# Neighbourhood attention over 16x8 column blocks with a bias laid out by the host

## The reference

```python
GRID_W, WIN_COLS, rows = 64, 16, 8        # 512 tokens are a grid of 8 rows x 64 columns; 16 heads of 64
q, k, v, g = split(h @ w_in)              # latent tokens; kc, vc from the context tokens
row_idx = clip(r - 4, 0, rows - 8)[:, None] + arange(8)      # with 8 rows: always all 8
col_idx = clip(col - 8, 0, 64 - 16)[:, None] + arange(16)    # 16 neighbouring columns
s_loc = q . k[row_idx, col_idx] + rpb[head, row_idx - r + 7, col_idx - col + 15]
s_ctx = q . kc
p = softmax(concat(s_loc, s_ctx))         # over 128 neighbours and 256 context tokens
o = p_loc . v[row_idx, col_idx] + p_ctx . vc
y = (o * silu(g)) @ w_out
```

## Time and profile before

| | us |
|---|---|
| median of 3 runs | 3138.78 (3133.11 to 3140.57) |
| the profiled execution: its time | 3141.7 |
| the profiled execution: its span | 3139.9 |
| PE busy | 2919.9 (93%) |
| DVE busy | 1757.9 (56%) |
| ACT busy | 970.3 (31%) |
| POOL busy | 803.6 (26%) |

### The profile page before, as it was taken

How to read it: one execution, slowest core, us unless ns; L and a number is a source line. 1 busy time by engine, 2 the same in 40 slices (tenths; PEclk the granted TensorE clock), 3 DMA queues, 4 the chain that set the end, 5 groups by cost and what they waited for, 6 DMA issues and landing times. The chain is left out here.

```text
span 3139.9 us, 37990 instructions
## 1 busy us (share of the span) xinstructions
PE 2919.9 (93%) x14938; PEld 2410.3 (77%) x14938; DVE 1757.9 (56%) x2601; ACT 970.3 (31%) x1552; POOL 803.6 (26%) x304
## 2 busy tenths in 40 slices
PE   7999999999998898888989999999999889999999
PEld 6776777777777776667868888888888668878887
DVE  4984766666645998976556566552233536431111
ACT  2223344444332222223234423122222334332222
POOL 0221212111134443431200022232222120134444
PEclk8998999999999999899989999999999899999999
DMA  5244332232124553432310033331111120022223
GB/s 209 84 148 122 99 93 92 73 99 73 65 101 168 167 168 113 142 114 73 104 58 1 1 101 108 119 104 64 63 61 61 46 81 1 21 74 94 96 98 101
DMA packets 110896, 287.38 MB, mean 92 GB/s; under 512 B 38720, under 2 KB 41888, under 8 KB 110208
## 3 DMA queue, kind: packets, MB, share of 16 engines
q1 hardware_dynamic: 108560, 281.03, 27.0%
q10 hardware_dynamic: 2160, 3.93, 0.4%
HBM read 278.90 MB, written 6.03 MB: 91 GB/s over the span
## 5 line engine op out<-in xcount | busy, mean ns | idle before, releaser
L705 POOL TENSOR_TENSOR w_lo<-w_raw,w_hi 128x1024 fp32r<-128x1024 f32 x300 | 803.4, 2679 | 2325.2 <-ACT w_hi L987 2325.1
L753 PE MATMUL turns<-h_hi,w_hi 128*128 128x512 f32 (+1 forms) x2480 | 811.0, 376 | 86.5 <-POOL w_lo L705 67.9
L753 PE MATMUL turns<-h_hi,w_lo 128*128 128x512 f32 (+1 forms) x2480 | 786.4, 366 | 0.0
L753 PE MATMUL turns<-h_lo,w_hi 128*128 128x512 f32 (+1 forms) x2480 | 784.0, 366 | 0.0
L753 PEld LDWEIGHTS turns<-h_hi,w_hi 128*128 128x128 f32 x2480 | 428.3, 194 | 202.7 <-POOL w_lo L705 89.4
L1204 DVE CUSTOM_DVE_ANT_0 ada_acc<-ada_raw,cond_rows,ada_bias 128x1024 f32<-128x1024 f32 x264 | 501.2, 1923 | 19.3 <-DMA ada_raw<-in_adapack 11.6
L753 PEld LDWEIGHTS turns<-h_hi,w_lo 128*128 128x128 f32 x2480 | 424.0, 193 | 76.3
L753 PEld LDWEIGHTS turns<-h_lo,w_hi 128*128 128x128 f32 x2480 | 425.4, 193 | 73.2 <-issue 1.4
L987 ACT ACTIVATE w_hi<-w_raw 128x1024 fp32r<-128x1024 f32 x300 | 315.4, 1051 | 407.0 <-PE turns L753 389.0
L1195 DVE SCALAR_TENSOR_TENSOR x_lat<-turns,modulation,x_lat 128x512 f32<-128x512 f32 x112 | 83.9, 749 | 413.7 <-PE turns L753 413.7
L753 PE MATMUL turns<-m_hi,w_lo 128*128 128x512 f32 (+1 forms) x768 | 233.4, 358 | 0.0
(11 more groups left out here) (199 smaller groups left out, 3585.1 us busy)
## 6 DMA issues: line engine op xcount, KB each, us to landing
w_raw<-in_wpack SPq DMA_DIRECT2D x300, 512.0 KB, 3.5
ada_raw<-in_adapack SPq DMA_DIRECT2D x176, 512.0 KB, 4.4
bias<-bias_table SPq DMA_DIRECT2D x32, 224.0 KB, 3.8
ada_first_a<-in_adapack SPq DMA_DIRECT2D x12, 512.0 KB, 8.7
bias_table<-bias_out ACTq DMA_DIRECT2D x16, 240.0 KB, 2.4
x_lat<-in_xT SPq DMA_DIRECT2D x1, 2048.0 KB, 8.6
x_ctx<-in_ctxT SPq DMA_DIRECT2D x2, 1024.0 KB, 8.8
ada_first_b<-in_adapack SPq DMA_DIRECT2D x4, 512.0 KB, 14.7
```

What stands on the lines that cost most here:

```text
L705: pool.tensor_tensor(Wl[:, b, :], RAW[:, b, :], Wh[:, b, :].bitcast(F32), ALU.subtract).then_inc(w_split, 1)
L753: ins = pe.matmul(dst[:, lo:lo + sz], w, x[:, lo:lo + sz], start=first and n == 0, stop=last and n == 2)
```

## The change

1. The q, k, v and g tiles of the NA layer are evicted in another token order: four column blocks, each 8 rows x 16 columns = 128 tokens (`by_rows` is the old order read, `by_cols` the new order written, runs of 16 elements). q and g take a copy more on ACT, through `tmp1`; k and v are evicted in two instructions for latent and context. The output goes back to row order when it is written to `o_hi`, `o_lo`.
2. A query tile is now a column block, and meets only the blocks that its windows reach: `NA_CHUNKS` gives 2 local blocks + 2 context chunks for tiles 0 and 3, 3 + 2 for tiles 1 and 2. Scores, softmax, transposes and P*V go over 512 or 640 keys and not over 768; in P*V a block that only one of the two query tiles meets is multiplied over 128 queries.
3. Context and local scores lie side by side, and the bias holds zeros for the context, so that one DVE instruction adds, negates and takes the minimum (that is, minus the maximum), and one ACT instruction takes the exponential and its sum.
4. The bias comes from the host in its final layout, 128 x 1792 floats per head. The 16 `bias_row` steps, the HBM table, the loads of `onehot` and `rpb` and all waits on them are gone. The load of a head is one transfer of 896 KB; before it was two of 224 KB. No other work takes the place of the `bias_row` steps between the `poolmix` steps.
5. `ada_acc` loses its second half: `bias1` gets a home of its own. In `cond_rows` the two condition rows pass one after the other through the one buffer; the thrown-away product of `ada_chunk` goes on top of `ada_raw`; for the first sections the context accumulator lies in the arena.

```diff
+NA_CHUNKS = ((4, 5, 0, 1), (4, 5, 0, 1, 2), (4, 5, 2, 3, 1), (4, 5, 2, 3))
+NA_PLACE = ((0, 1, 4, 5), (0, 1, 2, 4, 5), (4, 5, 1, 2, 3), (4, 5, 2, 3))
+NA_BIAS_AT, NA_BIAS_W = (0, 896, 256, 1280), 1792
...
-                if L == 0:
-
-                    for _ in range((0, 2, 2, 2, 2, 2, 3, 3)[m]):
-                        add("bias_row", g=len(rows) // 8, c=len(rows) % 8, st=len(rows) % 2, k=len(rows) + 1)
-                        rows.append(1)
...
+        def by_cols(ap):
+            return ap.rearrange("p (b r c) -> p r b c", b=4, r=ROWS, c=WIN)
+        def by_rows(ap):
+            return ap.rearrange("p (r b c) -> p r b c", b=4, r=ROWS, c=WIN)
+        def score_at(qt):
+            local = (len(NA_CHUNKS[qt]) - 2) * P
+            return (TX - local, TX - local, TX) if qt < 2 else (TX - TC, TX, TX - TC)
...
-                if s is last_gate0:
-                    sp.wait_ge(dve_done, s.d1)
-                    sp.dma_start(HOT[:], A["onehot"]).then_inc(hot_in, 16)
-                    sp.dma_start(RPB[:], A["rpb"]).then_inc(hot_in, 16)
...
-                        for r in range(2):
-                            sp.dma_start(BIAS[n % 2][r * 64:r * 64 + 64, :].rearrange("c (s j) -> c s j", j=GRID_W),
+                        sp.dma_start(BIAS[n % 2][:], A["bias"][n]).then_inc(bias_in[n % 2], 16)
...
+                        if s.na:
+                            _, at_l, at_c = score_at(s.qt)
+                            k0, nl = min(c for c in NA_CHUNKS[s.qt]) * P, (s.nk - 2) * P
+                            pe.matmul(SP_[:, 0, at_l:at_l + nl], x[:, q], y[:, k0:k0 + nl], start=n == 0, stop=n == 2)
+                            ins = pe.matmul(SP_[:, 0, at_c:at_c + TC], x[:, q], y[:, TX:TT], start=n == 0, stop=n == 2)
...
+                        wide = NA_CHUNKS[s.qt + 1 if s.qt == 0 else s.qt]
+                        for n, k in enumerate(wide):
+                            q = slice(0, 256) if n < 4 else slice(P, 256) if s.qt == 0 else slice(0, P)
+                            for j, (v, p) in enumerate(((Vh, PTh[0]), (Vh, PTl[0]), (Vl, PTh[0]))):
+                                ins = pe.matmul(PS[:, b, TT + q.start:TT + q.stop], v[:, k, :], p[:, n, q], start=n + j == 0,
...
                     for c in range(2):
-                        ins = act.activation(ACC[:, c, :], CROW[:, c, :], ACT.Tanh, scale=0.5)
-                    ins.then_inc(crow_tanh, 1)
+                        if c:
+                            act.wait_ge(crow_made, 2 * n - 1)
+                        act.activation(ACC[:], CROW[:, c, :], ACT.Tanh, scale=0.5).then_inc(crow_tanh, 1)
...
-                            act.activation(ex[:, 0:TX], ex[:, 0:TX], ACT.Exp, bias=st[:, 2:3], scale=1.0, accum_out=st[:, 3:4])
-                            give(act.activation(ex[:, TX:TT], SP_[:, 0, TX:TT], ACT.Exp, bias=st[:, 2:3], scale=1.0,
-                                                accum_out=st[:, 4:5]))
+                            give(act.activation(ex[:, 0:nk], ex[:, 0:nk], ACT.Exp, bias=st[:, 2:3], scale=-1.0,
+                                                accum_out=st[:, 3:4]))
...
-                        give(act.activation(Oh[r, s.tile, s.q0:s.q0 + 256], PVT[r, :], ACT.Copy))
+                        give(act.activation(blocks(Oh[r, s.tile, :], s.q0), paired(PVT[r, :]), ACT.Copy))
...
-                        give(act.activation(G2[:, s.pair % 2, :], ps[:, 0:t], ACT.Tanh, scale=0.5))
+                        act.activation(by_cols(T1[:, 0:TX]), by_rows(ps[:, 0:TX]), ACT.Copy)
+                        give(act.activation(by_cols(G2[:, s.pair % 2, :]), by_rows(ps[:, 0:t]), ACT.Tanh, scale=0.5))
...
+                        if s.ev == "k":
+                            act.activation(dst[:, TX:TT], ps[:, TX:TT], ACT.Copy)
+                            give(act.activation(by_cols(dst[:, 0:TX]), by_rows(ps[:, 0:TX]), ACT.Copy))
+                        else:
+                            chain(act.activation(by_cols(T1[:, 0:TX]), by_rows(ps[:, 0:TX]), ACT.Copy, scale=0.125))
+                            give(act.activation(dst[:, 0:TX], T1[:, 0:TX], ACT.Copy))
...
-                            dve.tensor_tensor_reduce(ex[:, 0:TX], SP_[:, 0, 0:TX], bias, 1.0, -3.0e38, ALU.add, ALU.max,
-                                                     st[:, 0:1])
-                            chain(dve.tensor_reduce(st[:, 1:2], SP_[:, 0, TX:TT], AX.X, ALU.max))
-                            give(dve.tensor_scalar(st[:, 2:3], st[:, 0:1], st[:, 1:2], -1.0, ALU.max, ALU.mult))
+                            give(dve.tensor_tensor_reduce(ex[:, 0:nk], SP_[:, 0, s0:s0 + nk], bias, -1.0, 3.0e38, ALU.add, ALU.min,
+                                                          st[:, 2:3]))
...
-                        if s.na:
-                            chain(tt(st[:, 5:6], st[:, 3:4], st[:, 4:5], ALU.add))
-                            chain(dve.reciprocal(st[:, 6:7], st[:, 5:6]))
+                        chain(dve.reciprocal(st[:, 6:7], st[:, 3:4]))
```

More of the change, by code:

```diff
@@ L205, in na_scores @@
     def na_scores(n, q, k):
-        sc[n] = add("scores", na=True, pair=n // 8, half=n % 8 // 4, qt=n % 4, st=0, eb=n % 2, first=n % 4 == 0, nk=NT)
+        sc[n] = add("scores", na=True, pair=n // 8, half=n % 8 // 4, qt=n % 4, st=0, eb=n % 2, first=n % 4 == 0, nk=len(NA_CHUNKS[n % 4]))
         sc[n].after = [q, k]
     def na_trans(n):
-        tr[n] = add("trans", na=True, eb=n % 2, col=n % 2 * P, nk=NT, qt=n % 4)
+        tr[n] = add("trans", na=True, eb=n % 2, col=n % 2 * P, nk=len(NA_CHUNKS[n % 4]), qt=n % 4)
         tr[n].after = [soft[n - 1]]
@@ L468, in plan @@
     for s in steps:
-        n = {"hnorm": 0, "back": 0, "rope": 1, "vtrans": 1, "scores": s.st, "bias_row": s.st, "trans": 1 if s.na else None}.get(s.kind)
+        n = {"hnorm": 0, "back": 0, "rope": 1, "vtrans": 1, "scores": s.st, "trans": 1 if s.na else None}.get(s.kind)
         if n is not None:
@@ L590, in build_blocks @@
         act_own, dve_own = sem("act_own"), sem("dve_own")
-        consts_in, x_in, hot_in = sem("consts_in"), sem("x_in"), sem("hot_in")
-        bias_out = [sem(f"bias_out{n}") for n in range(2)]
+        consts_in, x_in = sem("consts_in"), sem("x_in")
         bias_in = [sem(f"bias_in{n}") for n in range(2)]
@@ L801, in _ @@
                     unit(s)
[L802 to L808, removed]
                 elif s.kind == "adape":
@@ L906, in _ @@
                     k0 = NT - s.nk
-                    for n in range(s.nk):
+                    if s.na:
+                        wide = NA_CHUNKS[s.qt + 1 if s.qt == 0 else s.qt]
[3 more added lines that the diff above has]
+                                ins = pe.matmul(PS[:, b, TT + q.start:TT + q.stop], v[:, k, :], p[:, n, q], start=n + j == 0,
+                                                stop=n == len(wide) - 1 and j == 2)
+                    for n in range(0 if s.na else s.nk):
                         for j, (v, p) in enumerate(((Vh, PTh[s.pt]), (Vh, PTl[s.pt]), (Vl, PTh[s.pt]))):
@@ L1013, in _ @@
                     load_table(ACT.Sqrt)
-                if s.d0 and s.kind != "bias_row":
+                if s.d0:
                     act.wait_ge(dve_done, s.d0)
-                if s.a0 and s.kind != "bias_row":
+                if s.a0:
                     act.wait_ge(act_done, s.a0)
@@ L1118, in _ @@
                     m = s.m
-                    if s is first_xupd:
-                        for n in range(2):
-                            act.wait_ge(bias_out[n], 16 * 8)
                     if s.ev == "u":
@@ L1562, in constants, with bias_places @@
     return c
+def bias_places():
+    at = np.full((ROWS, WIN, NA_BIAS_W), NDR * NDC + 1)
+    for b in range(4):
+        local = sorted(c for c in NA_CHUNKS[b] if c < 4)
+        at0 = NA_BIAS_AT[b] + (0 if b < 2 else TC)
+        for n, chunk in enumerate(local):
+            for r in range(ROWS):
+                for c in range(WIN):
+                    q = b * WIN + c
+                    first = min(max(q - WIN // 2, 0), GRID_W - WIN)
+                    for rk in range(ROWS):
+                        for jc in range(WIN):
+                            j = chunk * WIN + jc
+                            ok = first <= j < first + WIN
+                            at[r, c, at0 + n * P + rk * WIN + jc] = (rk - r + 7) * NDC + j - q + 15 if ok else NDR * NDC
+    return at.reshape(P, NA_BIAS_W)
 def layout(i):
```

104 lines of the change are left out of this document (41 added, 63 removed).

## The result

| | before | after |
|---|---|---|
| median | 3139.68 us (3133.11 to 3143.65, 4 runs) | 3063.03 us (3055.68 to 3068.73, 4 runs) |
| the profiled execution: time, span | 3141.7, 3139.9 | 3068.73, 3066.9 |

A forecast was written before the change was run, and what follows sets the result against it. PE, busy 93% of the span, and its waits were taken as the bound. NA 54 + clock 4.5 + poolmix 16 - `cond_rows` 0.5 = 74 us off 3141.7: 3067.7, median 3065 (own range 3052 to 3078).

The forecast's parts named there:

- PE's own work in NA: NA: fewer keys shorten scores, P*V and transposes; narrow P*V taken at 0.12 us, bounds -6 and +12 us.
- Steps 2+3 and 6+7: NA, the steps of a pair with 768-token k and v units: PE-bound, 1.3 us less for each two.
- rival A: Narrow P*V at the float32 price, no clock gain, poolmix at 1.2 GHz: 53 us less, 3086 us; chance 0.14.
- The softmax chain: NA: fewer keys and merged instructions take 1.4 to 1.7 us off an even step, 0.95 to 1.25 off an odd one.
- Step 5: NA, sixth of a pair's eight steps: 0.7 us less, then PE's 4.6 us is the bound.
- The clock in NA: NA: waits shrink or move, so PE's clock rises; 4.5 us gained, bounds 0 and 10.
- What is added and hides: NA: extra q and g copies, runs of 16 elements and the larger bias load cost nothing; bias at most 2 us.
- rival C: NA: runs of 16 elements double the evictions, 28 us over eight pairs: 3093 us; chance 0.12.
- Poolmix: Poolmix without `bias_row` goes at DVE's 3.06 us per step; first xupd 16 us earlier, bounds 12 and 20.
- rival B: All goes well: narrow P*V at 0.06 us, clock gain 10, poolmix gain 20: 3050 us; chance 0.18.
- `cond_rows`: The condition rows still run in turn, with two more handoffs: 0.5 us lost in all, at most 2.
- Rivals D and E: D: nothing net, 3134 us, chance 0.05. E: less dense NA held at 1.2 GHz, 3348 for the whole stage, chance 0.03.

The follow-up runs named there:

- r2: Kernel after with PE's saved NA matmul work (scores, P*V, transposes) put back as useless matmuls: 3090.69 us, 0.9841 of before.
- r4: Kernel after with tokens left in row order, so no instruction has runs of 16 elements: 3065.88 us, 0.9765 of before.
- r1: Kernel before with only the host-made bias table (old layout) and no `bias_row` steps: 3121.51 us, 0.9939 of before.
- r5: Kernel after with useless matmuls in PE's pauses of the first poolmix stage: 3067.19 us, 0.9762 of before.
- r8: Kernel after with the edits of r5 and r6 and the step 1 part of r7 together: 3035.51 us, 0.9666 of before.
- r6: Kernel after with the `ada_chunk` of odd NA steps moved behind the softmax, ahead of the unit's eviction: 3043.36 us, 0.9690 of before.
- r7: Kernel after with useless matmuls ahead of step 1's transposes (3) and step 5's scores (5) in NA: 3054.63 us, 0.9729 of before.
- r3: Kernel after with the softmax unmerged again (old separate instructions) over the new, fewer keys: 3087.56 us, 0.9834 of before.

## Why the prediction was right, and where not

**PE's own work in NA.** Right. Steps 2+3 and 6+7 were to lose 1.3 and lost 1.31 and 1.41; r2 puts the work back and gets it back. The narrow P*V matmuls were taken at 0.12 and measured 0.093 (0.06, 0.12, 0.10), between the two bounds and 2.6 us in all below the value taken. The figure of the Trainium skill ("TensorE: Matmul & The Clock Gate", "Back-to-back issue gap"), 81 ns, was nearer than the row I chose. My upper bound, the float32 price that rival A took, is out.

**The softmax chain.** Right in steps 0 and 4 (1.5 and 1.0 for 1.5 and 0.8). Step 1 has the forecast number, 0.8, but partly by luck: without a half-clock stretch it lost 1.0 (6.92 to 5.96), with one only 0.2 (7.71 to 7.53), and the average came out because three of the six pairs have one where five had. Step 5 failed. It was to lose 0.7 and lost 0.1. At full clock it does what the prediction said: 5.38 in before (one pair of six) and 4.51 in after's first pair, 0.87 less, and then "PE's 4.6 is the bound". But in pairs 1 to 6 it starts at half clock. In before such a stretch cost 1.0 in step 5 (6.35 against 5.38), because part of it lay in a wait for the softmax; in after there is no wait left, PE is the bound, and it costs all of 1.6 (6.09 against 4.51). The last pair gave 11.1 for the 10 forecast, since its step 1 lost 1.6 and not 0.8: it had a half-clock stretch in before (7.70) and has none in after (6.10; in r4, where it has one, 7.61). That is luck too.

**The clock in NA** is the term that was wrong: a gain of 4.5 forecast, a loss of some 5 found. Before has 12 half-clock stretches in NA, after 10. In pairs 1 to 6, before has five in step 5 at 1.0 us each and five in step 1 at 0.8 (7.71 against 6.92), 9 us together; after has nine at 1.6, 14.4 together. The prediction took the shortfall of before as a stock that shrinks with the waits. The count did shrink a little; the price of each rose, since the slack that had covered part of it went. What made up for most of it is the narrow P*V (2.6), step 4 (0.2 x 7) and the last pair (1.1). The stretches of after hang on two pauses that the change leaves: `v_lo` in step 1, and the softmax behind the `ada_chunk` in step 4. The timeline of PE in after, a step 5 after a wait of 1.99 us:

```profile
471.09 0.63 PE L753 MATMUL turns<-h_hi,w_lo 128*128 128x512 f32 x1
471.52 0.63 PE L753 MATMUL turns<-h_hi,w_hi 128*128 128x512 f32 x1
...
474.08 0.41 PE L753 MATMUL turns<-h_hi,w_hi 128*128 128x512 f32 x1
474.32 0.39 PE L753 MATMUL turns<-h_lo,w_hi 128*128 128x512 f32 x1
```

**What is added and hides.** Right. Runs of 16 elements cost nothing (r4), so rival C is out. The bias load of 896 KB lands in a median of 4.6 us and nobody waits for it. The copies of q and g on ACT show nowhere in a step's length, though no run takes them away by themselves.

**Poolmix.** Right to 0.1 us in all, and within 0.4 along the way: allowing for the start at 233.6 instead of 229.1, the forecast put the multiplications of poolmix 2 and 7 at 247.3 and 263.3, and they are at 247.69 and 263.19; from the first poolmix matmul to the first xupd it is 45.6 before and 29.6 after. r1 gets the same 16 by itself. The clock was back sooner than the forecast had it, from 248.63 on, in the middle of poolmix 3. The upper bound of 20, which rival B took, is out: r5 keeps full clock all along and is only 1.3 us shorter there than after, since DVE's pace is the next bound. The Trainium skill's rule that spoke against this part ("TensorE: Matmul & The Clock Gate", "HAM oscillation — how this bites in real kernels") was read too widely. PE did start at half clock behind its 5.16 us of idle, but then the clock came back and stayed, with PE at work for only 2.1 of each 3.06 us. The page's own case has waits longer than the bursts between them; here they are 1 us, and the 12 us didn't come. One gain was missed: the first xupd unit ran at full clock and took 8.7 us from its first matmul to its first reader, and 11.2 in before. That is 2.5 more.

**`cond_rows`.** The first modulation row leads to `pool_scale` 0.3 us later; 0.5 was the forecast. The timeline of ACT, where the second tanh now waits for the product between:

```profile
73.28 1.06 ACT L1013 ACTIVATE ada_acc<-cond_rows 128x1024 f32<-128x1024 f32 x1 [1.29 <-DVE cond_rows L1198]
```

**The sum.** Forecast for the profiled execution 3067.7, measured 3068.73; for the median 3065, measured 3063.03. That is closer than the terms were, and so close by luck. NA gave 54.2 where 58.5 was asked for, the first xupd gave 2.5 unasked, the first stage was 4.5 us late, and the stages behind NA gave 5.4 that I had put at 0 ("everything from 1400 us on unchanged": from 1249 us of before on it is 5.6). The late start is no effect of the change: the eight kernels that share after's code up to there lie between -6.5 and +4.6 us at 222 us; the same work drifts that far. The last isn't explained. The variations of after gave between 1.0 (r8) and 9.5 (r2) there, r1 0.8, so I hold it for scatter of the same kind, but that is argued and not shown.

Rivals D and E are out as well. In E's direction the runs say more: the denser stage of r6, r7 and r8 has more clock, and it was r3, with longer pauses, that had less.

## What to carry to other kernels

A stretch at reduced clock behind a pause costs more once its step has become PE-bound, so a change that removes waits should be priced with the full length of such stretches, and not with what they cost while there was slack. After a change like this, look for the pause that is left and see what stands ahead of it in an engine's order: here one line that moves a reduction of 1.3 to 3.3 us behind the softmax, on DVE, gave 20 us more, because it ended the pause and the clock loss behind it. Before a difference of some us between two profiles is explained, compare the stages that the change doesn't touch: here identical work had drifted apart by up to 11 us after 222.

## What the runs showed of the hardware

- PE's pauses of 1.2 to 2.2 us in otherwise dense work can be followed by a stretch at 1.2 GHz (512-token matmuls 0.43 apart, not 0.23) worth 1.6 us where PE is the bound; behind r3's pauses of 2.70 us it was worth 3.1 (7.60 against 4.53). In step 5 of after it came in six pairs of seven, in step 1 in every other pair. Filling the pause with six or ten matmul records without use removed all of them (clock 0.95 to 1.00, r7). Why the same pause sometimes has none behind it stays open.
- PE at work for 2.1 of each 3.06 us kept its full clock in poolmix (matmuls of 768 tokens 0.35 apart from 248.63 us on).
- The reduction of a 128x1024 block on DVE lasts 1.28 us alone (r6) and 3.31 while POOL forms a `w_lo` (after). Whoever moves it to another time moves its price too.
- An fp32r matmul of 128 columns in a stream took 0.093 us on average, one of 256 columns 0.12, so half the width saved less than a quarter.
- A copy of 512 elements per partition in runs of 16 took the same 592 to 593 ns as in one run.
